# A new order for the steps of two mixer layers, with gate tiles between the steps of the sparse attention's output

## What is computed

```python
z = jnp.einsum('btd,dc->btc', xn, w_in)
(m_qk, m_v, m_o, m_if, s_q, s_ckv, i_q, i_k, i_w, d_q, d_k, d_v, g_pre) = _split_cols(z)
...
merged = (gates[:, :, 0] * jnp.einsum('btc,cd->btd', y_a, w_branch[0])
          + gates[:, :, 1] * jnp.einsum('btc,cd->btd', y_b, w_branch[1])
          + gates[:, :, 2] * jnp.einsum('btc,cd->btd', y_c, w_branch[2]))
x = x + jnp.einsum('btd,de->bte', merged, w_out)
```

## Time and profile before

| | us |
|---|---|
| median of 3 runs (2903.65 to 2913.78) | 2911.97 |
| the profiled execution, its own time | 2908.88 |
| span of the profiled execution | 2907.1 |
| TensorE busy in it | 2704.9 |
| VectorE busy in it | 1802.8 |
| ScalarE busy in it | 1177.7 |
| GpSimd busy in it | 231.9 |

### The profile page before, as it was taken

How to read it: one execution, slowest core, us unless ns; L and a number is a source line. 1 busy time by engine, 2 the same in 40 slices (tenths; PEclk the granted TensorE clock), 3 DMA queues, 4 the chain that set the end, 5 groups by cost and what they waited for, 6 DMA issues and landing times.

```text
span 2907.1 us, 29086 instructions
## 1 busy us (share of the span) xinstructions
PE 2704.9 (93%) x11636; PEld 2037.4 (70%) x11636; DVE 1802.8 (62%) x1938; ACT 1177.7 (41%) x1325; POOL 231.9 (8%) x112
## 2 busy tenths in 40 slices
PE   5997898989997889989989989799999999999997
PEld 4445546876445448888768879687878778787876
DVE  2045525442065345555555447699999989999997
ACT  1112311011113310034620014577777777777775
POOL 0000003320000013300024320000000000000000
PEclk9998899999997899999999999899999999999999
DMA  5441135532430145545445535498989989898985
GB/s 161 139 158 58 58 116 174 201 132 101 164 130 30 58 161 186 201 140 177 157 148 207 193 120 186 146 381 311 381 318 361 338 323 372 313 382 315 376 328 195
DMA packets 276201, 610.10 MB, mean 210 GB/s; under 512 B 12670, under 2 KB 50228, under 8 KB 275904
## 3 DMA queue, kind: packets, MB, share of 16 engines
q1 hardware_dynamic: 276032, 607.64, 59.0%
HBM read 606.56 MB, written 1.05 MB: 209 GB/s over the span
## 4 chain that ended last, share of the span: by engine, by line
PE 83%; DVE 12%; ACT 3%; issue 1%; SPq 0%; DMA 0%; DVEq 0%; ACTq 0%
PE bank L418 81%; DVE split L1455 5%; PE bank L448 2%; PE bank L637 1%; DVE parts L1501 1%; ACT xs L1077 1%; DVE x_resid L1483 1%; DVE work L1712 0%; ACT split L1077 0%; DVE parts L1441 0%; DVE top L1711 0%; DVE tmp L1491 0%; ACT parts L1077 0%; SPq L2044 0%; ACT L1077 0%
## 5 line engine op out<-in xcount | busy, mean ns | idle before, releaser
L418 PE MATMUL bank<-split,parts 128*128 128x512 f32 (+1 forms) x6720 | 1539.7, 389 | 29.3 <-DVE parts L1441 13.1
L418 PEld LDWEIGHTS bank<-split,parts 128*128 128x128 f32 x6720 | 1247.7, 189 | 291.5 <-issue 19.8
L1455 DVE TENSOR_TENSOR split<-ring,split 128x2048 fp32r<-128x2048 f32 x444 | 1024.5, 2353 | 95.2 <-POOL split L2025 67.7
L1077 ACT ACTIVATE split<-ring 128x2048 fp32r<-128x2048 f32 x336 | 641.8, 1918 | 194.9 <-PE bank L418 194.9
L418 PE MATMUL bank<-ring,xnT 128*128 128x512 f32 (+1 forms) x1024 | 428.9, 578 | 1.8 <-ACT xnT L1077 1.8
L418 PEld LDWEIGHTS bank<-ring,xnT 128*128 128x128 f32 x1024 | 194.3, 192 | 234.2 <-issue 231.9
L2025 POOL TENSOR_SCALAR split<-ring 128x2048 fp32r<-128x2048 f32 x108 | 231.7, 2148 | 1477.6 <-DVE x_resid L1483 1114.3
L1077 ACT ACTIVATE parts<-bank 128x512 fp32r<-128x512 f32 x150 | 79.7, 583 | 390.5 <-PE bank L637 390.5
L1501 DVE TENSOR_TENSOR parts<-bank,parts 128x512 fp32r<-128x512 f32 x150 | 95.4, 678 | 144.3 <-ACT parts L1077 144.3
L1077 ACT ACTIVATE tmp<-bank 128x512 f32<-128x512 f32 x158 | 87.6, 586 | 203.6 <-PE bank L418 203.6
L1491 DVE TENSOR_TENSOR tmp<-bank,tmp 128x512 f32<-128x512 f32 x150 | 97.8, 679 | 115.7 <-PE bank L418 114.8
(11 more groups left out here) (233 smaller groups left out, 1619.9 us busy)
## 6 DMA issues: line engine op xcount, KB each, us to landing
ring<-in_moe_w_gate SPq DMA_DIRECT2D x112, 1024.0 KB, 7.9
ring<-in_moe_w_up SPq DMA_DIRECT2D x112, 1024.0 KB, 7.5
ring<-in_moe_w_down SPq DMA_DIRECT2D x112, 1024.0 KB, 7.5
ring<-in_w_gate_up SPq DMA_DIRECT2D x44, 1024.0 KB, 5.2
ring<-in_w_in SPq DMA_DIRECT2D x40, 1024.0 KB, 6.3
ring<-in_ret_w_in SPq DMA_DIRECT2D x24, 1024.0 KB, 5.1
ring<-in_w_down SPq DMA_DIRECT2D x22, 1024.0 KB, 5.0
ring<-in_w_in SPq DMA_DIRECT2D x24, 876.0 KB, 5.8
```

The lines of the kernel that those rows point to most:

```text
L418: return nc.tensor.matmul(o, l, r, start=first, stop=final, **kw)
L1077: return nc.scalar.activation(out, in_, func, **kw)
L1455: V.tensor_tensor(split[:, m % SPLITS, 1, :], ring[:, n % RING, :], split[:, m % SPLITS, 0, :].bitcast(F32), ALU.subtract).then_inc(low_ma ...
```

## The change

It changes the order of the steps in the two layers, on every engine, and the cut of z.

- `w_if`, its two loads and its product go. The six chunks of 438 columns become chunks of 440 (the last 436) that begin at the gate rows' columns, so the first holds the input and forget gates and most of the sparse q. Their 8 columns are brought into rows by four products of z with the identity.
- Each chunk of z has its own point, so VectorE and ScalarE begin on it as it comes. TensorE's order is now: qk, ckv, index chunk, transposes of ckv, if/sq chunk, kv product, gate rows, index transposes, v, index scores, o, transposes of sparse q and k, dq, sparse scores, dk, dv, **the first tile of gate 1, then the six steps of the sparse output with the other three tiles of gate 1 between the first of them**, the mLSTM's weights, transposes of the sparse output and of the differential heads, branch 1, the mLSTM's values, the two chunks of gate 0, the mLSTM's transposes, the differential scores, the two chunks of gate 2, the differential outputs, branch 0, the transposes, branch 2.
- The merge is taken in three parts (1, 0, 2), each behind its branch. The sigmoids are taken as the gate and o tiles leave PSUM.
- SyncE streams the units in the new order. The mLSTM's rows have new places in `ybuf`.

The core of the diff, TensorE first:

```diff
-        z_chunks = [(C_V, 512), (C_O, 512)] + [(C_SQ + 438 * i, 438) for i in range(6)]
-        g_chunks = [(C_G + 512 * i, 512) for i in range(6)]
+        z_v, z_o = (C_V, 512), (C_O, 512)
+        z_if_sq, z_ckv, z_index, z_dq, z_dk, z_dv = [(C_IF + 440 * i, min(440, C_G - C_IF - 440 * i)) for i in range(6)]
...
-                b = fill(ALL)
-                for g in range(2):
-                    for k in range(KT):
-                        ins = mm(bank[b][0:4, g * SEQ:(g + 1) * SEQ], w_if[:, li, k, 4 * g:4 * g + 4], xnT[:, k, :],
-                                 k == 0, k == KT - 1)
-                hand(ins, b, "dve")
...
+                def gate_tiles(branch):
+                    for i in range(2):
+                        views = [take((4, 512)), take((4, 512))]
+                        for tt in range(TT):
+                            b = fill(ALL)
+                            bias = 6 * li + 2 * branch + i
+                            mm(bank[b][:, :], ident[0:12, bias:bias + 1].broadcast_to([12, P]), bgate[:, :], True, False)
+                            for k in range(KT):
+                                ins = mm(bank[b][:, :], xn_tile(k, tt), views[k // 4][:, k % 4, :], False, k == KT - 1)
+                            hand(ins, b, "act")
+                            if tt == 1:
+                                read_by(for_act, 2)
+                            yield
+                    point("gates")
...
+                columns(z_ckv, "ckv")
+                columns(z_index, "index")
                 eng.wait_ge(kvn_dve.sem, pe.next(kvn_dve))
                 transposes(lambda i: yb[:, i % 2, (i // 2) * P:(i // 2 + 1) * P], 4, "dve")
                 point("ckvT")
+                columns(z_if_sq, "sq")
...
+                eng.wait_ge(act_freed.sem, pe.point("sq", act_freed))
+                b = fill(ALL)
+                for g in range(2):
+                    for tt in range(TT):
+                        c = g * SEQ + tt * P
+                        ins = mm(bank[b][0:4, c:c + P], zc(tt, C_IF + 4 * g, 4), ident, True, True)
+                hand(ins, b, "dve")
...
+                columns(z_v, "v")
...
+                columns(z_o, "o")
+                turn_heads(lambda tt, c: zc(tt, C_SQ + c, P), lambda tt, c: kv[:, tt, c:c + P])
+                columns(z_dq, "dq")
+                head_scores(0)
+                columns(z_dk, "dk")
+                columns(z_dv, "dv")
+
+                def turn_probs(j):
+                    eng.wait_ge(prob_act.sem, 12 * li + j + 1)
+                    transposes(lambda i: pbuf[:, j, i * P:(i + 1) * P], 4, "act")
+                    point("pT")
+
+                between = gate_tiles(1)
+                next(between)
+                turn_probs(0)
+                for j in range(6):
+                    tt, _, hs = score_bank(j)
+                    if j < 5:
+                        turn_probs(j + 1)
+                    if j < 4:
+                        next(between, None)
+                    if j in (0, 2):
+                        bo = fill(ALL)
+                    eng.wait_ge(act_freed.sem, pe.point("pT", act_freed))
+                    for i, h in enumerate(hs):
+                        for s in range(tt + 1):
+                            c = (i * (tt + 1) + s) * P
+                            ins = mm(bank[bo][:, h * HD:(h + 1) * HD], pT[:, j % 2, c:c + P],
+                                     kv[:, s, HALF + h * HD:HALF + (h + 1) * HD], s == 0, s == tt)
+                    if j in (1, 5):
+                        hand(ins, bo, "dve")
+                point("dsa")
+                mlstm_weights()
+                eng.wait_ge(dve_freed.sem, pe.point("dsa", dve_freed))
+                turn_branch()
+                turn_heads(lambda tt, c: zc(tt, C_DQ + c, P), lambda tt, c: zc(tt, C_DK + c, P))
+                branch(1)
+                mlstm_values()
+                gates(0)
+                eng.wait_ge(yb_dve.sem, pe.next(yb_dve))
+                turn_branch()
+                head_scores(2)
+                gates(2)
+                eng.wait_ge(act_freed.sem, pe.point("dv", act_freed))
+                for tt in range(TT):
+                    bo = fill(ALL)
+                    for jj in range(tt + 1):
+
+                        eng.wait_ge(diff_dve.sem, pe.next(diff_dve))
+                        transposes(lambda i: pbuf[:, 2 * (tt + jj), i * P:(i + 1) * P], 4, "act")
+                        point("pT")
+                        eng.wait_ge(act_freed.sem, pe.point("pT", act_freed))
+                        for i in range(4):
+                            h = i if tt == 0 else 2 * jj + i // 2
+                            s = 0 if tt == 0 else i % 2
+                            ins = mm(bank[bo][:, h * P:(h + 1) * P], pT[:, (tt + jj) % 2, i * P:(i + 1) * P],
+                                     zc(s, C_DV + h * P, P), s == 0, s == tt)
+                    hand(ins, bo, "dve")
+                branch(0)
+                eng.wait_ge(yb_dve.sem, pe.next(yb_dve))
+                turn_branch()
+                branch(2)
...
+                z_evac(*z_dq)
                 exps()
-                gates(gates_after["dsa"])
+                z_evac(*z_dk)
+                z_evac(*z_dv)
+                head_roots(8, 24)
+                gate = C_G + 2 * HALF
+                tile = iter([(0, 0), (1, 0), (0, 1), (1, 1)])
+
+                def gate_tile():
+                    tt, i = next(tile)
+                    b = take()
+                    A(zc(tt, gate + i * HALF, HALF), b[:, :], ACT.Sigmoid).then_inc(act_freed.sem, act_freed.tick())
+
+                gate_tile()
                 for j in range(6):
                     copy(pT[:, j % 2, :])
+                    if 0 < j < 4:
+                        gate_tile()
+
+                eng.wait_ge(dve_freed.sem, act.point("floor", dve_freed))
+                A(floor[:, 1, :], floor[:, 0, :], ACT.Exp).then_inc(floor_act.sem, floor_act.tick())
+                for h in range(M_HEADS):
+                    eng.wait_ge(dve_freed.sem, act.point("exponents", dve_freed))
+                    A(pbuf[:, h, 0:384], pbuf[:, h, 0:384], ACT.Exp).then_inc(decay_act.sem, decay_act.tick())
                 evac_features(None, yT[:, 1, :, :], (0, 1))
+                turned_heads(2)
+                roots(hsum[:, 2, kY:kY + 8], hsum[:, 1, kY:kY + 8])
+                gates(0)
+                evac_features(G_MN + 4 * li, yT[:, 0, :, :], (0, 1))
                 exps()
-                gates(gates_after["diff"])
+                gates(2)
...
+                mlstm_scans()
+                eng.wait_ge(act_freed.sem, dve.point("dq", act_freed))
+                z_sums(((1, (C_DQ, 8, HD)),))
+                eng.wait_ge(act_freed.sem, dve.point("dk", act_freed))
+                z_sums(((2, (C_DK, 8, HD)),))
+                mean_squares(z_heads(1, 8, 24), z_heads(0, 8, 24), HD)
+                z_inverse(8, 24)
+                rope_from_z(C_DQ, 1)
+                rope_from_z(C_DK, 2)
...
+                mlstm_weights()
+                merge(1, True)
+                mlstm_values()
...
+                merge(0, False)
+                ins = merge(2, False)
...
-            for li in range(DEPTH):
-                load(w_if[:, li, :, :], a["w_in"][li, :, C_IF:C_IF + 8].rearrange("(k p) c -> p k c", p=P))
...
                 columns(w_in, C_QK + 512)
-                for col, width in z_chunks:
+                for col, width in (z_ckv, z_index, z_if_sq):
                     columns(w_in, col, width)
-                gate_columns(gates_after["z"])
                 rows_of(a["dsa_w_kv_up"][li], 1)
-                gate_columns(gates_after["kv"])
-                gate_columns(gates_after["mlstm"])
-                gate_columns(gates_after["dsa"])
-                gate_columns(gates_after["diff"])
-                gate_columns(len(gates))
-                for br in range(3):
-                    rows_of(a["w_branch"][li, br], 2)
+                for col, width in (z_v, z_o, z_dq, z_dk, z_dv):
+                    columns(w_in, col, width)
+                gates(1)
+                branch(1)
+                gates(0)
+                gates(2)
+                branch(0)
+                branch(2)
                 rows_of(a["w_out"][li], 4)
```

More of the change, by code:

```diff
@@ L45 @@
 HALVES = 4
-PARAMS = 24
+PARAMS = 22
 GROUPS = D_FF // HALF
@@ L718, in layer, with columns, gates @@
                     point("qk")
[L719 to L731, removed]
+                def columns(z_chunk, name=None):
+                    chunk(z_chunk[1], "act")
+                    if name:
+                        point(name)
+                def gate_tiles(branch):
[12 more added lines that the diff above has]
+                    point("gates")
+                def gates(branch):
+                    for _ in gate_tiles(branch):
+                        pass
+                columns(z_ckv, "ckv")
+                columns(z_index, "index")
```

(48 more changed lines are left out.)

257 lines of the change are left out of this document (88 added, 169 removed).

## The result

The changed kernel takes 2802.8 us (median of four runs, 2802.3 to 2803.1). The ratio to the kernel before is 0.963, with a 95% interval of 0.962 to 0.965. The forecast was 2810 and the range 2797 to 2843. The profiled execution has a span of 2800.5 us, 106.6 less than before.

A forecast was written before the change was run, and what follows sets the result against it. TensorE, busy 93% of the span, was taken as the bound. Eleven terms gave 96.6 us over two layers, the start 5: 2908.9 less these is 2807.3, plus 3.1 for the median, 2810 (range 2797 to 2843).

The forecast's parts named there:

- term 3: mLSTM values and output: two gate chunks cover the output-norm wait, products take 3.5 us; gain 10.5 us a layer.
- term 5: Wait for a bank held by the top-k chain: covered by dense work, tightest margin some 3 us; gain 6.6 a layer.
- term 9: Wait for the differential norm: lies under branch 0's 14 us; gain 5.7 us a layer.
- term 10: The three branches: 44.2 us become 42.4 at a gate tile's rate; gain 1.7 us a layer.
- rival B: A covered wait shows after all because VectorE is late: about 6 us a layer, 2822, up to 2840; chance 0.10.
- Term 4: Transposes and index scores: 13.9 us become 11.1, 24 transposes behind the mLSTM weights taking 4.2; gain 2.8 a layer.
- Term 7: Sparse output: 17.9 us become 10.3, with gate tiles between steps covering evacuations; gain 7.6 us a layer.
- Term 11: mLSTM weights: stay at 14.2 us, still falling to half clock on the way, bounds 9.1 and 18.2; gain 0.
- Rival A: Clock falls in the attention's tail, stays at half through the mLSTM: 9 us a layer, 2828; chance 0.20.
- Term 1: w_if product goes, eight columns and four small products are added: net gain 5.8 us in each layer.
- The start: Initial parameter wait: without the two w_if loads TensorE starts at about 15 us; gain 5, once, between 2.3 and 8.
- rival D: Clock follows alternating dense tiles and small steps, staying at half through the gates after: slower, 3024; chance 0.03.

The follow-up runs named there:

- Experiment 2: Changed kernel with the mLSTM's values placed behind the two gate 0 chunks instead of ahead of them: 2832.6 us, ratio 0.975.
- Experiment 1: Changed kernel with the four gate 1 tiles in one block ahead of the sparse output, none between its steps: 2804.2 us, ratio 0.966.
- Experiment 8: Changed kernel with sparse scores behind the dv chunk, making probabilities late; gate tiles still between the sparse-output steps: 2801.9 us, ratio 0.965.
- experiment 9: Changed kernel with sparse scores behind the dv chunk, one gate tile ahead of the six steps, three in a block behind: 2819.2 us, ratio 0.971.
- experiment 7: Changed kernel with gate 0's tiles between the heads of the mLSTM weights, differential scores and gate 2 covering their old place: 2793.1 us, ratio 0.962.
- experiment 4: Changed kernel with w_rt as the first parameter load, not the last: 2798.5 us, ratio 0.964.
- experiment 3: Changed kernel with SyncE waiting for the parameters before issuing the first ring loads: 2800.1 us, ratio 0.964.
- experiment 5: Changed kernel with the two w_if loads put back, unused: 2799.9 us, ratio 0.964.
- experiment 6: Changed kernel with parameter loads split over two semaphores, the second group waited for behind the first q/k features: 2793.7 us, ratio 0.963.
- experiment 10: Changed kernel with tiles between mLSTM-weight heads, split parameter loads, and differential transposes one step ahead of their products: 2783.3 us, ratio 0.959.

## Why the prediction was right, and where it was not

The direction, the size and the place of the gain were right: 101.6 us worked out, 106.6 measured in the profiled executions. By its steps:

- Terms 2, 3, 5, 6, 8, 9, 10 (waits covered, and half clock behind them gone): the waits that these terms took away are gone, and every product there ran at full clock. The short ones that the prediction kept are still there (three of 0.7 at the differential outputs, 0.9 and 1.5 about the last branch). Experiment 2 took the cover of term 3 away and got back the wait and the half clock behind it, so for term 3 the cause is shown. For the bank wait of term 5 and the norm wait of term 9 the trace shows only that they are gone with dense work in their place; no experiment took that away again. No wait for a bank appeared, so the margin of term 5 sufficed and rival B did not come.
- Term 4: the 24 transposes behind the mLSTM weights took 4.2 us as priced. Terms 3 and 10 were 0.7 and 0.9 too small: the mLSTM's values took 2.8 us instead of 3.5, the three branches 41.5 instead of 42.4.
- Term 7's gain was sized 2.1 us too small, and its reason was half wrong. The six steps cost 8.2 us net of the tiles (179.77 to 220.03 less four tiles of 8.0), not 10.3. I gave the credit to the tiles between the steps. Experiment 1 shows that in this order they save 0.6 us in the layer: what cured the sparse output was the head start of the top-k and the scores, so that no 3.2 us wait stands in it. Experiments 8 and 9 show that the tiles are insurance: 10.4 us in the first layer if the probabilities are late.
- Term 11: 14.2 taken, 14.3 measured. The clock falls inside the mLSTM in every order tried without tiles there, as the term had assumed. Rival A, half clock from the attention's tail through the whole mLSTM, did not come: sparse-output steps without a long wait do not bring the clock down.
- Term 1: 5.8 a layer was right for the removed work, but the 2.4 us of half clock in the second layer did not fall on the next products, which ran at full clock from 607.7. In the first layer 2.0 did, where there were none before. That, with the 2.4, is why the second layer gained 4.4 more. It is chance and not the order: of the traces whose instructions are the same up to there, four (experiments 1, 7, 8, 9) have this first product at full clock (27.9 us) and three (the changed kernel twice, experiment 2) at half for a part of it (29.6 to 29.9); in experiments 2 and 4 the second layer's product took 30.2.
- The start is the step that failed: -5 forecast, +1.5 measured, and 0 to +1.6 over the seven traces with these loads. It took w_if's rows as the work that delayed w_rt, because they were the same kind and issued before it. Experiments 3 to 5 show instead that the last of the small loads lands at 18.8 us or later in any order, and experiment 6 that the loads which are in by 12.5 us suffice to start. What keeps the small loads until then was not settled. Between 14 and 18 us the DMA engines are reported busy throughout (share 0.95 before, 1.01 after), and yet move only 87 and 73 GB/s. It is not the ring: in experiment 3, where no ring load is issued before 19.1, the same stretch shows 0.98 and 75 GB/s, so the parameter loads alone fill it.
- What was not run is the removal of the w_if product alone; its 7.0 and 9.4 us are the lengths of its rows before.
- Rivals C and D: no transfer was late, and the clock never oscillated around the interleaved steps. Experiment 8 kept 1.00 with small steps between dense tiles. The Trainium skill's page "TensorE: Matmul & The Clock Gate", section "A second HAM failure mode: psum-queue depth-cycling", says of one bf16 kernel that frequent short idles of TensorE between groups of products, as it cycles through PSUM banks, made the clock swing between its levels. No run here shows that: the differential outputs with their waits of 0.7 us kept 1.00 after the change as before.

## What to carry to other kernels

Put dense work behind the product that starts a vector chain, not behind the wait for the chain: that moved 22 us of waits and most of the half clock behind them out of each layer, and taking one such cover away cost 14.1 us for a wait of 10.1. Interleaving dense tiles with small steps was worth 0.6 us while the operands were early, and about 10 us a layer when they were late, so first ask which it is. A semaphore that counts all loads starts the kernel at the last and least of them: split it by first use. And a difference of 2 to 3 us in one place can be a clock phase that comes out otherwise in the next execution: compare it with other traces of the same instructions before explaining it.

## What was not expected

- Which small products lower the clock. The six steps (64-column products and transposes) kept 1.00 for 8.5 us after the last dense tile. The mLSTM's weights, where products with four rows stand between those of q and k, brought it down 3 to 4 us after they began, in the kernel before (240.5 to about 244.5), in the changed one (220.0 to about 224) and in experiment 1 (218.1 to about 221.5), while TensorE was never idle. In experiment 9 it took 5.5 us (228.9 to about 234.4). Which of these products does it, no run shows. One gate tile (8 us) between heads kept the heads at full clock, though a part of one tile ran at half (8.8 us in experiment 7, 8.7 in experiment 10).
- Clock phases differ between executions of the same instructions. The first q/k product of experiment 1 and of the second trace of the changed kernel, with nothing different ahead of it:

```profile
34.97 27.86 PE L416 MATMUL bank<-xnT,ring 128*128 128x256 f32 x128 [1.02 <-ACT xnT L1106]
34.05 29.58 PE L416 MATMUL bank<-xnT,ring 128*128 128x256 f32 x128 [1.02 <-ACT xnT L1109]
```

  The router product, some 800 us behind the last edited step, took 7.0 us before and in experiments 2, 3 and 5, and 4.2 to 4.6 in all others. With one trace of nearly every kernel, an effect of an edit on it cannot be told from chance.
- The two loads of w_if (rows of 32 bytes) could be left out or put back without moving the start (20.3, 20.1 us).
